# The order of TensorE's products inside a chunk of the expert value table (one core, Trainium2)

## What is computed

```
out = einsum('chk,chkd->cd', w, expert_v[ec])     # w = gate * gelu(token . expert_u[ec])
```

## Time and profile before

| what | value |
|---|---|
| median of 3 runs | 1959.64 us (1958.53 to 1961.08) |
| span of the profiled execution, first to last instruction | 1956.3 us |
| PE, PEld busy | 1943.5 us (99%), 1736.1 us (89%) |
| DVE, ACT, POOL busy | 1665.8 (85%), 1122.3 (57%), 658.4 us (34%) |
| HBM traffic over the span | 289 GB/s |
| granted TensorE clock | full in all 40 slices of the span |
| chunks of the v table | from 1363.5 us to the end |

### The profile page before, as it was taken

How to read it: one execution, slowest core, us unless ns; L and a number is a source line. 1 busy time by engine, 2 the same in 40 slices (tenths; PEclk the granted TensorE clock), 3 DMA queues, 4 the chain that set the end, 5 groups by cost and what they waited for, 6 DMA issues and landing times.

```text
span 1956.3 us, 32644 instructions
## 1 busy us (share of the span) xinstructions
PE 1943.5 (99%) x11722; PEld 1736.1 (89%) x11722; DVE 1665.8 (85%) x2524; ACT 1122.3 (57%) x1588; POOL 658.4 (34%) x408
## 2 busy tenths in 40 slices
PE   9999999999999999999999999999999999999999
PEld 8899989998988888999999999999777777777776
DVE  8777778777888777999999999988888888888897
ACT  7665556555677455666565665655545455555554
POOL 0301110111000001877777877685222221223220
PEclk9999999999999999999999999999999999999999
DMA  6745654566455556999999999999999999999997
GB/s 235 256 163 193 199 193 159 188 204 194 160 175 190 183 185 228 332 342 341 329 352 327 338 338 356 329 377 365 337 370 376 373 373 379 375 375 379 365 382 266
DMA packets 137575, 566.50 MB, mean 290 GB/s; under 512 B 44008, under 2 KB 52080, under 8 KB 88112
## 3 DMA queue, kind: packets, MB, share of 16 engines
q1 hardware_dynamic: 87296, 414.05, 57.9%
q0 software_dynamic: 49936, 149.49, 22.9%
q10 hardware_dynamic: 288, 2.36, 0.3%
HBM read 548.31 MB, written 16.88 MB: 289 GB/s over the span
## 4 chain that ended last, share of the span: by engine, by line
PE 92%; DVE 3%; DMA 2%; ACT 1%; issue 1%; SPq 0%; DVEq 0%; ACTq 0%
PE psum L925 27%; PE psum L902 17%; PE psum L617 15%; PE psum L907 11%; PE psum L621 8%; PE psum L603 3%; PE psum L602 3%; PE psum L607 3%; ACT whi L479 1%; DVE wlo L487 1%; PE psum L797 1%; DVE xr L487 1%; DMA arena<-v_rows 1%; PE psum L979 0%; DMA raw<-u_cols 0%
## 5 line engine op out<-in xcount | busy, mean ns | idle before, releaser
L473 DVE TENSOR_TENSOR wlo<-raw,whi 128x1024 fp32r<-128x1024 f32 x242 | 296.1, 1231 | 112.1 <-PE psum L621 74.6
L902 PE MATMUL psum<-xr,whi 128*128 128x384 f32 x2048 | 380.9, 337 | 0.2 <-ACT whi L479 0.2
L925 PE MATMUL psum<-whi,xr 128*128 128x512 f32 x1512 | 363.8, 389 | 1.7 <-DVE xr L1859 1.1
L902 PEld LDWEIGHTS psum<-xr,whi 128*128 128x128 f32 x2048 | 351.2, 188 | 0.6 <-ACT whi L479 0.3
L925 PEld LDWEIGHTS psum<-whi,xr 128*128 128x128 f32 x1512 | 283.4, 188 | 63.0 <-DVE xr L1859 1.7
L479 ACT ACTIVATE whi<-raw 128x2048 fp32r<-128x2048 f32 x168 | 320.8, 1910 | 23.8 <-DMA raw<-v_rows 15.7
L617 PE MATMUL psum<-xr,whi 128*128 128x512 f32 x1296 | 330.1, 397 | 0.4 <-issue 0.4
L466 ACT ACTIVATE whi<-raw 128x1024 fp32r<-128x1024 f32 x244 | 250.3, 1053 | 100.4 <-DMA raw<-stream 44.0
L1364 POOL DMA_INDIRECT arena<-v_rows,small x64 | 139.7, 2183 | 407.2 <-DVE arena L1823 404.4
L617 PEld LDWEIGHTS psum<-xr,whi 128*128 128x128 f32 x1296 | 232.3, 189 | 44.3 <-issue 0.8
L487 DVE TENSOR_TENSOR wlo<-raw,whi 128x1024 fp32r<-128x1024 f32 (+1 forms) x126 | 197.5, 1572 | 27.0 <-issue 21.2
(11 more groups left out here) (282 smaller groups left out, 3202.0 us busy)
## 6 DMA issues: line engine op xcount, KB each, us to landing
raw<-stream SPq DMA_DIRECT2D x244, 512.0 KB, 3.3
raw<-v_rows SPq DMA_DIRECT2D x85, 1024.0 KB
raw<-u_cols SPq DMA_DIRECT2D x84, 1024.0 KB
arena<-v_rows SPq DMA_DIRECT2D x43, 1024.0 KB
arena<-u_cols SPq DMA_DIRECT2D x42, 1024.0 KB
gates<-arena POOLq DMA_DIRECT2D x8, 1536.0 KB, 9.7
small<-gates SPq DMA_DIRECT2D x62, 192.0 KB
arena<-x_t SPq DMA_DIRECT2D x4, 544.0 KB, 7.2
```

The lines of the kernel that those rows point to most:

```text
L473: nc.vector.tensor_tensor(wlo[:, k % 2 * HALF:(k % 2 + 1) * HALF], raw[:, s * HALF:(s + 1) * HALF], f(whi[:, s * HALF:(s + 1) * HALF]), AL ...
L902: mm(bank(at, 0, 2 * TD), hi_w[:, c * P:(c + 1) * P], z_all[:, :, c, 0:TD // TS, :], start=c == 0, stop=False)
L925: last = mm(at[:, (b * 4 + j * 2 + n) * 512:(b * 4 + j * 2 + n + 1) * 512], weights, src, start=begin, stop=end, skip_group_check=True)
```

## The change

In chunks 1 to 122 the order of TensorE's 20 products changes; nothing is added or removed. After the four upper products of the first 128 tokens now stand the wait for the lower table rows and the eight products with them (first tokens, then last 64). Behind those stand the wait for the lower weights and the eight products that use them. `half_done` is raised by the two last pairs, now those of `Wboth`.

```
                 part(0, 0, psum, Whi[q][:, 0:P], False, first, False)
                 if not first:
                     part(0, 1, psum, Whi[q][:, 0:P], False, False, False)
+                if not first and idle is None and residual is None:
+                    pe.wait_ge(lo_done, base * 2 + 2 * F_V + 2 * c + 2)
+                    for j in range(2):
+                        part(0, j, psum, Whi[q][:, 0:P], True, False, False)
+                    for j in range(2):
+                        part(1, j, psum[0:TS, :], Whi[q][:, P:TD], True, False, False)
+                    pe.wait_ge(w_lo, base + c + 1)
+                    for j in range(2):
+                        part(0, j, psum, Wlo[q][:, 0:P], False, False, True)
+                    for j in range(2):
+                        part(1, j, psum, Wboth[q], False, False, True).then_inc(half_done, 1)
+                    return
                 pe.wait_ge(w_lo, base + c + 1)
```

## The result

The changed kernel takes 1969.24 us (median of 5 runs, 1966.63 to 1973.20), the kernel before 1959.64 us: a ratio of 1.0048, 95% interval 1.0036 to 1.0060, that is 9.6 us slower. One execution of the kernel before took 6126.63 us and is no part of this comparison. The forecast was 1966.2 us. The profiled execution's span went from 1956.3 to 1967.2 us, by 10.9.

The account below looks back on a forecast made before the run. TensorE bounds the kernel, busy 524.37 of 525.00 us. Pairs 4.0, edge chunks 0.7, opening 1.9, given back -1.0 make 5.6; plus 1.0 for loads, 6.6 us on 1959.6: 1966.2 us, range 1960 to 1974.

Parts of the forecast that it names:

- Direction and mechanism: Slower: the lower-row wait moves from 2.72 to 0.91 us into a chunk, losing 1.81 us of cover.
- Release and threshold: Restart after the lower-row wait takes 0.16 us; TensorE stalls if the subtraction ends over 0.75 us into the chunk.
- Rival 1: Stalls smaller, release 0.06 us, edge cases vanish: 3.9 us or less, 1959.6 to 1963.5 us; chance 0.19.
- Waits before, 7.4 us: Waits at product line L925 in the kernel before, summed over all chunks from its profile view: 7.4 us.
- Pairs of row sums: VectorE row sums in two chunks running, ten places: nine cost 0.44 us each, 4.0 us together.
- Opening: Chunk 6's late subtraction makes chunk 7 start 1.86 us later, chunks 1, 2 and 5 included: 1.9 us.
- Late landings: Table loads: 1.0 us given back near 1585 us, 1.0 us added for stalls passed on through loads.
- The other bound: Chunk-by-chunk case with load landings fixed from their issue, so stalls are passed on: 9.5 us, against 5.6 with fixed times.
- rival 3: Landings follow their issue and the slow product spacing spreads: up to 13.9 us, 1973.5 us; chance 0.15.
- Spacing: Eight products per chunk run at 0.231 rather than 0.227 us: taken as 0, bounds -4.4 to +4.4 us.
- likeliest case: The forecast itself, stalls of 3.9 to 10 us, own range 1963.5 to 1969.6 us; chance 0.60.
- Signs asked of the profile: L925 idle time ended by subtractions grows from 2.6 to 8 to 12 us; the wait at 1585 us shrinks.

Follow-up runs that it names:

- e1: Kernel before with its old product order, only the wait for the lower table rows moved from behind product 12 to behind product 4: 1974.48 us, ratio 1.0073.
- e12: Second run of the old product order with the lower-row wait behind product 4, beside the changed kernel: 1974.88 us, ratio 1.0064.
- e10: Changed kernel with row sums on 256 of 2048 columns and plain 256-column loads in place of the v-row gathers: 1958.50 us, ratio 0.9996.
- e6: Changed kernel with the 64 gathers of v rows replaced by plain loads of 256 columns, row sums at full length: 1965.67 us, ratio 1.0043.
- e2: Kernel before with products grouped by weight tile as in the changed kernel, both waits at their old places: 1959.58 us, ratio 0.9999.
- e11: Changed kernel unaltered, measured a second time on the same chip as e12: 1974.0 us, ratio 1.0064, +13.1 us against the kernel before.

## Why the prediction was right, and which term was not

- **Direction and mechanism: right, and shown.** The cover that the wait loses is what costs: e1 and e12 show the whole cost with the wait alone, and e10 leaves none from chunk 7 on.
- **Release and threshold: right.** Chunk 17's 0.47 us against 1.18 - 0.91 leaves 0.19 us for the release, 0.16 was taken. The 0.76 of a single row sum sits at the edge as said: chunks 10 to 16 show 0.01 to 0.03. Rival 1 (a release of 0.06, the time within 0.2%) is out.
- **Waits before, 7.4 us: read too high.** The view counts PE's and PEld's idle time both; the chunks' excess was 2.7 + 1.1 = 3.8 us. No term of the sum rests on it.
- **Pairs of row sums, 4.0 us: right in size, but not all there.** e6 shows 3.9. In the changed kernel some were free, since a stall a few chunks ahead had already moved TensorE back: chunk 28 takes 4.61 us, three chunks after the stall of 25. The nine sum to 3.0 us. Chunk 64 (0.3 us) is a row-sum stall that has no term.
- **Opening, 1.9 us: right**, measured 4.3 - 2.7 = 1.6.
- **Late landings, 0 us in sum: the failed term.** I had them give back 1.0 us and cost 1.0 us. Measured in the traces: chunks 7 to 124 have 11.3 us, of which 3.0 are pairs, 0.3 is chunk 64 and 0.5 are edges, so late DMA and its followers make 7.5; before they made 1.1. That is +6.4 us where the prediction had 0. The wrong step is "at 98% busy the first is nearer": it followed one execution's late landings at fixed times, and found them hidden behind a TensorE that was already late. They are not fixed. In the execution after, other loads were late (for chunks 24, 31, 35, 48, 70, 84 and 92, by 0.7 to 1.5 us), and each late one costs about all of its lateness beyond 0.42 us (0.75 less the 0.33 that the subtraction needs anyway). I also left out the follower: one late chunk before a row sum is a new pair. The other bound, landings fixed from their issue, had 9.5 us and was nearer by its number alone: what it assumes, that stalls make loads late, is not what the trace shows (see rival 3).
- **Spacing, 0 between -4.4 and +4.4: right.** e2 and e10. The part of rival 1 in which runs of one tile spare reloads is out with them.
- **The number: partly luck.** The traced terms add up to 11.9 us and not 6.6. The 1969.24 us lie just inside the likeliest case's own 1963.5 to 1969.6; the second measurement's +13.1 us lie beyond its 10.
- **Rival 3 (feedback through the loads): not as described.** SyncE's wait for subtractions is 460.9 us in the 535 us from 1405 to 1940, before 453.9 in 525, the same share, and ScalarE's waits for table rows fell from 23.1 to 7.5 us. That fits with stalls that give the loads more time, which no run tests alone; what was left of lateness was no longer covered.
- **Signs asked of the profile.** The 8 to 12 us of idle time ended by subtractions were 30.1 (both PE rows added, and the landings); the wait near 1585 us didn't shrink, it came as chunk 48's. The subtraction ended over 0.75 us into its chunk in 45 of the 122 chunks, before in 84.

```profile
SPq L529 <- DVE wlo L487: 246.5, 57, 5.4
SPq L529 <- DVE xr L487: 214.4, 57, 4.6
```

## What to carry to other kernels

When a wait is moved forward, compare the cover left with all lateness that the trace shows now, including what is hidden at no cost: 48 chunks here were over 1.0 us late before and all but five of them cost nothing, because the last-needed operand was also waited for last. Random lateness (DMA at 98%) must be priced by its usual size and number, not by the places where one execution had it, and each late step should be followed one chunk on, where the helper engine's next long step passes it on. On an engine with a strict order of work, the operand that is made last should be used last.

## What the runs showed of the hardware

A wait of about two microseconds can cost twice. Chunk 5's wait for the subtraction lasts the same 2.27 us (PE) in the changed kernel and in e1, but the granted clock behind it differs. The changed kernel, by stretches (PE, PEld, DVE, ACT, POOL, clock, DMA share, GB/s):

```profile
1388.00:1391.00 3.00, 0.90 (x4) 0.76 (x5) 3.00 (x3) 1.97 (x3) 0.65 (x1) 1.00 0.53 134
1391.00:1394.40 3.40, 3.40 (x17) 2.56 (x16) 3.40 (x3) 0.30 (x2) 1.55 (x1) 1.00 0.98 371
```

And e1, whose wait ends at 1392.10:

```profile
1390.00:1393.00 3.00, 0.90 (x4) 0.77 (x5) 3.00 (x3) 1.98 (x3) 0.65 (x1) 1.00 0.62 164
1393.00:1396.40 3.40, 3.40 (x11) 2.20 (x10) 3.40 (x3) 0.00 (x0) 1.55 (x1) 0.55 0.99 371
1396.40:1400.00 3.60, 3.60 (x17) 2.94 (x16) 1.27 (x3) 2.32 (x3) 1.73 (x1) 0.95 0.73 269
```

After the same idle time the engine makes 17 products in 3.4 us in one execution and 11 in the other, at a granted clock of 1.00 and 0.55 (mostly the lower level, 1.2 GHz for 2.4 GHz). Chunk 5 then takes 8.70 and not 7.14 us: 1.56 us more. The same happened after the same wait in e6 and in e12 (8.69 us; in e12 the mean clock is 0.88 from 1386 to 1400 us) and, after a wait of 1.78 us, in chunk 45 of e1. In e11 it didn't, after 2.27 us, nor in chunk 115 of e1, after 1.77 us. So such a wait may or may not lower the clock, also within one kernel: of e6's six runs the two with a mean clock of 0.998 took 1969.53 and 1969.89 us, the four with 0.999 or 1.000 took 1964.12 to 1965.90. e1's six runs are ordered so too (1967.90 to 1973.55 us at 1.000, 1975.41 to 1979.16 below it), but e11's and e12's are not, so the clock is at most a part of what sets the executions apart. The Trainium skill ("TensorE: Matmul & The Clock Gate", section "What's actually happening") has a gate that lowers the clock when the engine was idle. The trace agrees that the clock falls behind an idle stretch, and shows that the length of the wait alone doesn't decide it.
